# Moving TensorE's activation operands by 16 and 112 bytes within a partition

## The reference, cut to what matters

```python
# first block
mod = silu(c) @ mod_w + mod_b
h = modulate(rms_norm(x), shift, scale)
y = gla_mixer(h, h_ctx, ...)                 # q, k, v, r = split(h @ w_in)
x = x + gate * rms_norm(y)
x = x + gate2 * rms_norm((silu(h2 @ wg) * (h2 @ wu)) @ ffn_w_out)   # hidden width 2816
# second block
proj = (x * (1 + scale) + shift) @ w_in_2    # qkv, z, beta, a, band q, k, v, gates
o_a = gated_deltanet(...)                    # 8 heads, chunks solved by a triangular solve
o_b = chunk_band_attention(q_b, k_b, v_b, rel_bias)                 # 16 heads of 64
x = layernorm(ALPHA * x + gate_t * ((gate_a * (o_a @ wa) + gate_b * (o_b @ wb)) @ w_o))
u = causal_dwconv(h @ w_up, conv) + b
x = layernorm(ALPHA * x + gate_f * ((silu(u_gate) * u_val) @ w_down))
```

## Time and profile before

| | |
|---|---|
| median of 3 runs | 1054.53 us (1053.82 to 1057.23) |
| the profiled execution | 1053.46 us, its span 1051.4 us |
| PE busy | 974.7 us (93%), 8430 matmul records |
| PEld busy | 913.3 us (87%) |
| DVE busy | 712.2 us (68%) |
| ACT busy | 555.8 us (53%) |
| POOL busy | 25.3 us (2%) |
| transfers | 196.78 MB, mean 187 GB/s |
| chain that ended last | PE 81%, DVE 9%, ACT 5%, DMA 3%, issue 1% |

### The profile page before, as it was taken

One profiled execution on the slowest core, in us unless ns is written; L12 is line 12 of the kernel. 1 busy time (PEld: TensorE's weight loads), 2 busy tenths in 40 slices (PEclk: granted clock), 3 DMA queues, 4 the chain that ended last, 5 costly groups with the idle time before them and its releaser, 6 DMA issues.

```text
span 1051.4 us, 19867 instructions
## 1 busy us (share of the span) xinstructions
PE 974.7 (93%) x8430; PEld 913.3 (87%) x8430; DVE 712.2 (68%) x1117; ACT 555.8 (53%) x838; POOL 25.3 (2%) x70
## 2 busy tenths in 40 slices
PE   5897999979999999799999999989998699999995
PEld 1477999869999999699798999888898599999994
DVE  2669947557777775698865543556568678888744
ACT  2658521545544533765745342656764466766433
POOL 2010000000000000210100000000000000000000
PEclk9898999998999999899999999999999889999997
DMA  9742775446888878347433436443356636556931
GB/s 328 229 130 80 244 256 186 164 137 209 284 267 287 287 264 278 138 144 248 155 121 103 145 119 170 141 157 126 120 195 213 233 103 192 182 188 191 334 96 40
DMA packets 57400, 196.78 MB, mean 187 GB/s; under 512 B 6096, under 2 KB 10592, under 8 KB 57056
## 3 DMA queue, kind: packets, MB, share of 16 engines
q1 hardware_dynamic: 51840, 187.72, 53.7%
q10 hardware_dynamic: 5216, 7.53, 2.5%
q0 software_dynamic: 256, 0.26, 0.1%
HBM read 194.43 MB, written 1.06 MB: 186 GB/s over the span
## 4 chain that ended last, share of the span: by engine, by line
PE 81%; DVE 9%; ACT 5%; DMA 3%; issue 1%; SPq 0%; ACTq 0%; DVEq 0%
PE panel_banks L401 68%; DMA raw<-in_panels 3%; DVE w_lo L1481 2%; PE work_banks L786 2%; ACT w_hi L969 1%; PE work_banks L614 1%; PE work_banks L573 1%; DVE raw L1514 1%; PE work_banks L715 1%; PE work_banks L757 1%; PE work_banks L546 1%; PE work_banks L869 1%; PE panel_banks L454 1%; PE work_banks L488 1%; PE work_banks L814 1%
## 5 line engine op out<-in xcount | busy, mean ns | idle before, releaser
L401 PE MATMUL panel_banks<-act_hi,w_hi 128*128 128x256 f32 (+1 forms) x1600 | 463.4, 290 | 23.6 <-DVE w_lo L1481 9.1
L401 PE MATMUL panel_banks<-act_hi,w_lo 128*128 128x256 f32 (+1 forms) x1600 | 455.0, 284 | 0.0
L401 PE MATMUL panel_banks<-act_lo,w_hi 128*128 128x256 f32 (+1 forms) x1600 | 455.0, 284 | 0.0
L1481 DVE TENSOR_TENSOR w_lo<-raw,w_hi 128x1024 fp32r<-128x1024 f32 x260 | 315.4, 1222 | 154.7 <-ACT w_hi L969 153.8
L969 ACT ACTIVATE w_hi<-raw 128x1024 fp32r<-128x1024 f32 x260 | 272.1, 1055 | 150.2 <-PE panel_banks L401 127.7
L401 PEld LDWEIGHTS panel_banks<-act_hi,w_hi 128*128 128x128 f32 x1600 | 304.8, 190 | 36.0 <-issue 20.1
L401 PEld LDWEIGHTS panel_banks<-act_lo,w_hi 128*128 128x128 f32 x1600 | 305.6, 191 | 1.9 <-issue 0.5
L401 PEld LDWEIGHTS panel_banks<-act_hi,w_lo 128*128 128x128 f32 x1600 | 304.8, 191 | 1.4
L401 PE MATMUL panel_banks<-hidden_hi,w_hi 128*128 128x256 f32 x352 | 98.6, 280 | 2.5 <-ACT hidden_hi L1186 2.5
L401 PE MATMUL panel_banks<-hidden_hi,w_lo 128*128 128x256 f32 x352 | 98.4, 279 | 0.0
L401 PE MATMUL panel_banks<-hidden_lo,w_hi 128*128 128x256 f32 x352 | 98.2, 279 | 0.0
(11 more groups left out here) (275 smaller groups left out, 1021.4 us busy)
## 6 DMA issues: line engine op xcount, KB each, us to landing
raw<-in_panels SPq DMA_DIRECT2D x356, 512.0 KB, 5.0
mix_work<-delta_rows ACTq DMA_DIRECT2D x2, 1024.0 KB, 10.8
x_t<-in_x ACTq DMA_DIRECT2D x1, 1024.0 KB, 9.2
gla_work<-in_ctx_x ACTq DMA_DIRECT2D x1, 1024.0 KB, 14.1
mix_work<-in_rel_bias ACTq DMA_DIRECT2D x1, 1024.0 KB, 9.9
out_x<-ffn_work SPq DMA_DIRECT2D x4, 256.0 KB, 2.5
mix_work<-in_rel_bias ACTq DMA_DIRECT2D x1, 768.0 KB, 13.9
c_wide<-in_c_rows ACTq DMA_DIRECT2D x1, 512.0 KB, 16.7
```

Source lines behind the costliest of these rows:

```text
L401: ins = pe.matmul(out_, a, b, start=start and p == 0, stop=stop and p == 2, skip_group_check=True)
L1481: dve.tensor_tensor(wlo[:, v_ % PARTS, :], raw[:, u % RAW, :], whi[:, v_ % PARTS, :].bitcast(F32), ALU.subtract)\
```

## The change

`act_hi` and `act_lo` become two slices of one buffer that is 32 bytes longer than both, and start 16 bytes later than before. `band_q` and `band_k` become slices of a second such buffer over the same bytes, 16 bytes later as well. Everything laid behind is thereby 32 bytes later. `hidden_hi` and `hidden_lo` become slices of one buffer with 128 bytes of spare room and start 80 bytes into it, so 112 bytes later than before.

```diff
         with ExitStack() as scope:
-            hhi = sb("act_hi", [P, 16, T], F32R, scope)
-            hlo = sb("act_lo", [P, 16, T], F32R, scope)
-        sb("under_hi", [P, KT, T])
-        bq = sb("band_q", [P, KT, T])
-        sb("under_lo", [P, KT, T])
-        bk = sb("band_k", [P, KT, T])
+            both = sb("act_parts", [P, 32 * T + 8], F32R, scope)
+            hhi, hlo = (both[:, n + 4:n + 4 + 16 * T].rearrange("p (a b) -> p a b", b=T) for n in (0, 16 * T))
+        under = sb("under_parts", [P, 32 * T + 8])
+        bq, bk = (under[:, n + 4:n + 4 + 8 * T].rearrange("p (a b) -> p a b", b=T)
+                  for n in (8 * T, 24 * T))
...
         with ExitStack() as scope:
-            fhi = sb("hidden_hi", [P, FT, T], F32R, scope)
+            hidden = sb("hidden_parts", [P, 2 * FT * T + 32], F32R, scope)
+            fhi, flo = (hidden[:, n + 20:n + 20 + FT * T].rearrange("p (a b) -> p a b", b=T)
+                        for n in (0, FT * T))
             cparts = fhi[:, 0, 0:32].rearrange("p (a b) -> p a b", b=4)
-            flo = sb("hidden_lo", [P, FT, T], F32R, scope)
             take = arena("ffn_work", 14000, scope)
```

## The result

Over seven runs each the changed kernel took 1060.66 us (1058.55 to 1063.32) and the kernel before 1056.19 us (1053.41 to 1057.77): a ratio of 1.0054, 95% interval 1.0035 to 1.0074. It is slower by half a per cent, where 2.2% less was forecast. The profiled executions lie further apart than the medians: 1061.2 against 1051.4 us of span.

What follows compares the result with a forecast made beforehand. TensorE was taken as the bound, through the distance between L401 matmuls (68% of the chain). 1053.46 less 22.4 from L401's operands, nothing from the rest, gave 1031.1 us profiled and 1031.5 as the median; range 1006 to 1079.

Steps and rivals of the forecast that it cites:

- the two levels: L401 matmuls start either 113.4 or 117.8 ns apart, 4.4 ns between the levels and nothing between them.
- part (2): VectorE and panel transfers feeding a faster TensorE: room enough, cost nothing, with margins of 15.4 us and some 70 GB/s.
- part (3): Work areas 32 or 160 bytes later, used by VectorE, ScalarE and plain float32 matmuls: nothing, 3 us either way.
- the Trainium skill's figure of 109.2 ns: Skill's time for a 256-column matmul; if the change restored it, the estimate would be 46 us off.
- part (1): L401's operands: an odd distance in 16-byte units brings 5600 slow matmuls to the fast level, 22.4 us gained.
- Slower: Rival: L401's moving stream off multiples of 64 meets the weight load more often; 122.2 ns, 1078 us, chance 0.24.
- Nothing changes: Rival: L401's level is not a matter of address but of how a burst begins; 1053 to 1056 us, chance 0.15.
- a burst that ran fast and slow with the same operands: Sign for no change: 60 matmuls at 518.60 us run fast with act tiles that run slow in the long stages.
- More than the fast level: Rival: L401 distances fall to 108 to 111 ns; 1001 to 1020 us, chance 0.10.

Runs made afterwards that it cites:

- e15: Kernel before with weights, act and hidden 16 bytes off a multiple of 64, both operand distances 192 modulo 256: 1039.48 us, ratio 0.9841.
- e3: Kernel before with only the work areas at the change's places, hidden moved by 128 bytes: ratio 0.9967.
- e7: Kernel before with a spare tensor of 128 bytes ahead of act, moving all behind it: ratio 0.9905.
- e4: Kernel before with weights, act and hidden all moved 16 bytes off a multiple of 64 (modulo 128): 1042.47 us, ratio 0.9868.
- the last group of runs: Kernel before with spare room of 128, 256 or 384 bytes, or weights and activations moved together, to test distances modulo 256: ratios 0.9841 to 0.9996.
- e14: The kernel with 128 bytes of spare room ahead of act, run a second time, against the kernel before: ratio 0.9903.
- e6: Kernel before with weights moved by 16 bytes, everything behind them, act and hidden too, by 128: ratio 1.0059.
- the first four experiments: Against the kernel before: act and bands moved; hidden moved; work areas moved; weights, act and hidden all 16 bytes off: ratios 1.0030, 1.0019, 0.9967, 0.9868.
- e2: Kernel before with only hidden moved, by 112 bytes, to the change's very bytes: ratio 1.0019.
- e5: Kernel before with act and hidden 32 bytes further (modulo 128), weights unmoved: 1064.27 us, ratio 1.0080.

## Why the prediction was wrong

**What bounds it, and the two levels:** right. L401's distance is the number that carries the result, about 9 of the 9.8 us of the profiled pair, and part (2) (what feeds TensorE has room) and part (3) (the work areas cost nothing) held: e15 runs all five long stages at the fast level with the same transfers and VectorE work, and e3 moved the areas without a loss. That the Trainium skill's figure of 109.2 ns would come back ("TensorE: Matmul & The Clock Gate", section "Wait — 56ns, not 53.3ns?") was not seen in any stage of any run; 113.3 is the lowest level that held.

**The step that failed** is in part (1): "In units of 16 bytes the distance between a matmul's two operands is even before and odd after", and from it "I take the fast level, because both kinds of operand reach it in the trace and it is the nearest row below". The places of the two operands to each other do set the levels, which is as far as I was right. But the reading of odd as good came from no row, since every distance in the trace before was 64 modulo 128 and none other. The rows I took for evidence showed which levels exist at that one distance. They could not show that another distance would select among the same two; it replaced them by 118.3 to 120.1. So the fast level that some 520 matmuls had was lost, and the slow one got slower by 0.5 to 2.3 ns: the term put at 22.4 us gained was about 9 us lost. What does bring the fast level back is 192 modulo 256, a shift of 128 bytes (e7), which no row before could show for the long stages. The rows on the GLA values held a hint of it, at that distance and fast in two pieces of four, that the prediction took for a sign that any kind of operand can reach the level.

**The rivals.** "Slower" had the right mechanism in part, a moving stream that meets the weight load worse, and put its price at 24.5 us where 4.5 was measured, 9.8 in the profiled pair: 122.2 ns was priced, and 119.2 on average came. But it gave as its reason a run that no longer begins on a multiple of 64, and e4 and e15 refute that. "Nothing changes" cited a burst that ran fast and slow with the same operands; that observation was sound and is what the last group of runs explains in part: the distance modulo 256 sets how likely the fast level is, and e7 and e14 differ in a stage with nothing changed. The Trainium skill's rule that stood with it (the same page, section "Step-by-step: what each phase is for": a weight load takes nothing from the running matmul) does not agree with these runs as far as distances between the two operands change the pace: of what L401 reads, e6 and e7 differ in the place of the weights alone, and the fast level is gone in e6. Whether a port's bandwidth is what is short, no run here shows. "More than the fast level" is not there. The range held 1060.66 us; the direction and the size were wrong.

**Why the measured loss is smaller than the profiled one.** The kernel before is not steady: its 25 runs beside the first four experiments went from 1050.85 to 1059.32 us. One long stage at the other level is 4.6 us, and e7 and e14 show that such levels can differ between executions of one program; that this makes the spread of the kernel before is likely, but only profiled executions show levels. The profiled execution of before was one of the quicker ones (1053.46 against a median of 1056.19), and that of the changed kernel one of its slowest (1063.24 against 1060.66).

**Left open.** Which memory or port the two streams share was not isolated; no run took the weight load away. Why a stage keeps the level that it fell into, and what about its first matmuls chooses it, is not shown. That the second hidden stage wants the 16 bytes rests on three kernels with one profile each. No kernel had weights and `act` off by 16 at a distance of 64 in more than one profile, so what the 16 bytes do for the act stages is open.

## What to carry to other kernels

Where a kernel is bound by float32r matmuls with a fresh stationary operand each, take the distance between starts from the trace, look for separate levels, and try the start addresses of the two operands against each other: here the start addresses were worth 2.4% between the worst and the best layout (1064.27 us in e5, 1039.48 in e15) with no instruction changed. A trace in which all large tensors start alike says nothing of how another alignment would do, in either direction; a spare tensor of 64, 128 or 256 bytes is a cheap way to ask. And two kernels that are the same in a stage may still differ there by 2 us (`qkv` before and in e2), so a small gain is to be read in the levels of the stages before it is put down to the edit.

## What the runs showed of the hardware

- A float32r matmul of 128 x 128 by 256 columns, with its own weight load, has a fast and a slow level at the full clock, 113.3 and 117.8 ns, each reached within about six matmuls in the stages looked at and kept until TensorE next waits. The fast one was seen in long stages only where moving less stationary start is 64 modulo 128 bytes. With both starts 16 bytes off a multiple of 64 the slow one is 118.3.
- At other distances (0, 48, 68, 72, 80, 96 modulo 128) the long stages stood between 117.8 and 120.3 ns, with distances between starts that repeat in short patterns, such as 117, 124, 116, 123.
- At 192 modulo 256 the fast level held in 22 of 22 of the first four stages of the table, and through 3 of 5 of `branch` and `mix`; at 64 modulo 256 the same act stages were fast in 2 of 15, and `branch` and `mix` in none of 5. With weights moving it was 14 of 20 pieces at 192 and 4 of 20 at 64.
- At the granted clock of 0.50 the changed layout cost nothing: 213 ns a matmul before (23 in 4.90 us), and six in 1.28 us after, from the first of these starts to the second:

```profile
852.83 0.41 PE L401 MATMUL panel_banks<-act_parts,w_lo 128*128 128x256 f32 x1
...
854.11 0.41 PE L401 MATMUL panel_banks<-act_parts,w_lo 128*128 128x256 f32 x1
```
- Plain float32 matmuls stayed at 216 ns a record (32 in 6.91 us) in all 17 profiles, and VectorE's and ScalarE's 1024-element steps at 1222 to 1223 and 1054 to 1056 ns.
